# Seven block products in place of eight in the up projections of a streaming encoder

## What is computed

```
def conv_gated_mlp(xn, w_up, conv_w, conv_b, w_down):
    gate, val = jnp.split(xn @ w_up, 2, axis=-1)          # 1024 -> 2 x 2816
    return (jax.nn.silu(causal_dwconv(gate, conv_w, conv_b)) * val) @ w_down

h = h + conv_gated_mlp(rmsnorm(h, norm_ffn_g[layer]), ...)
```

## Time and profile before

| | |
|---|---|
| median of three runs | 1069.85 us |
| the profiled execution's own time | 1069.4 us |
| its span (first to last instruction) | 1067.6 us |
| TensorE (PE), busy share of the span | 99% |
| VectorE (DVE) | 59% |
| ScalarE (ACT) | 44% |
| GpSimd (POOL) | 17% |
| TensorE's granted clock | 0.999 of full speed |

### The profile page before, as it was taken

One profiled execution on the slowest core, in us unless ns is written; L12 is line 12 of the kernel. 1 busy time (PEld: TensorE's weight loads), 2 busy tenths in 40 slices (PEclk: granted clock), 3 DMA queues, 4 the chain that ended last, 5 costly groups with the idle time before them and its releaser, 6 DMA issues.

```text
span 1067.6 us, 15530 instructions
## 1 busy us (share of the span) xinstructions
PE 1057.9 (99%) x5552; PEld 866.9 (81%) x5552; DVE 631.7 (59%) x876; ACT 464.9 (44%) x733; POOL 184.8 (17%) x245
## 2 busy tenths in 40 slices
PE   9999999999999999999999999999999999999997
PEld 8887778888888888888888777888888888888886
DVE  6798755666666666633335774756666666643332
ACT  6456664544344444422323665554443444422221
POOL 8998911300000000000000221310000000000000
PEclk9999999999999999999999999999999999999999
DMA  6551025133222222223233111322222222222322
GB/s 231 168 128 41 14 91 197 61 130 106 98 97 85 97 94 98 99 99 118 98 111 135 61 60 41 118 99 98 87 97 93 96 98 98 98 99 99 119 80 79
DMA packets 36460, 107.27 MB, mean 100 GB/s; under 512 B 7809, under 2 KB 10113, under 8 KB 36161
## 3 DMA queue, kind: packets, MB, share of 16 engines
q1 hardware_dynamic: 36416, 106.69, 29.4%
HBM read 102.09 MB, written 3.15 MB: 99 GB/s over the span
## 4 chain that ended last, share of the span: by engine, by line
PE 95%; DVE 2%; ACT 1%; SPq 1%; DMA 1%; issue 1%; POOL 0%; DVEq 0%; ACTq 0%
PE bank L1596 30%; PE bank L1597 29%; PE bank L1598 29%; PE bank L1620 2%; PE bank L1986 1%; PE bank L1963 1%; DMA raw<-wstream 1%; PE bank L1743 1%; PE bank L1808 1%; DVE ssum L1090 0%; SPq L360 0%; PE bank L1707 0%; PE bank L1687 0%; DVE wlo L1057 0%; PE bank L1771 0%
## 5 line engine op out<-in xcount | busy, mean ns | idle before, releaser
L1596 PE MATMUL bank<-xhi,whi 128*128 128x512 f32 x960 | 376.1, 392 | 0.2 <-DVE wlo L1057 0.2
L1597 PE MATMUL bank<-xlo,whi 128*128 128x512 f32 x960 | 373.7, 389 | 0.0
L1598 PE MATMUL bank<-xhi,wlo 128*128 128x512 f32 x960 | 373.6, 389 | 0.0
L1057 DVE TENSOR_TENSOR wlo<-raw,whi 128x1024 fp32r<-128x1024 f32 x177 | 224.7, 1271 | 206.6 <-ACT whi L702 206.2
L702 ACT ACTIVATE whi<-raw 128x1024 fp32r<-128x1024 f32 x177 | 187.2, 1058 | 324.0 <-PE bank L1598 300.4
L1596 PEld LDWEIGHTS bank<-xhi,whi 128*128 128x128 f32 x960 | 180.2, 188 | 39.6 <-issue 0.8
L1598 PEld LDWEIGHTS bank<-xhi,wlo 128*128 128x128 f32 x960 | 180.2, 188 | 37.8
L1597 PEld LDWEIGHTS bank<-xlo,whi 128*128 128x128 f32 x960 | 180.3, 188 | 36.9 <-issue 0.2
L1596 PE MATMUL bank<-ahi,whi 128*128 128x512 f32 (+1 forms) x374 | 141.0, 377 | 0.0
L1598 PE MATMUL bank<-ahi,wlo 128*128 128x512 f32 (+1 forms) x374 | 140.8, 377 | 0.0
L1597 PE MATMUL bank<-alo,whi 128*128 128x512 f32 (+1 forms) x374 | 140.8, 377 | 0.0
(11 more groups left out here) (264 smaller groups left out, 1051.5 us busy)
## 6 DMA issues: line engine op xcount, KB each, us to landing
raw<-wstream SPq DMA_DIRECT2D x177, 512.0 KB, 3.2
xin<-xT SPq DMA_DIRECT2D x8, 256.0 KB, 5.7
raw<-wstream SPq DMA_DIRECT2D x8, 256.0 KB, 5.2
h<-xT SPq DMA_DIRECT2D x1, 2048.0 KB, 8.3
u_scratch<-uperm SPq DMA_DIRECT2D x1, 1024.0 KB, 5.6
uc<-u_scratch SPq DMA_DIRECT2D x8, 128.0 KB, 4.4
bandsb<-band SPq DMA_DIRECT2D x1, 1024.0 KB, 4.7
outT<-outb SPq DMA_DIRECT2D x2, 512.0 KB, 2.8
```

The costliest lines, as they stand in the source:

```text
L1057: V.tensor_tensor(wlo[:, t % RING, :], raw[:, t % RAWS, :], whi[:, t % RING, :].bitcast(f32), ALU.subtract).then_inc(lo_done, 1)
L1596: MM(dst, wh, rhi, start=start, stop=False)
L1597: MM(dst, wh, rlo, start=False, stop=False)
L1598: return MM(dst, wl, rhi, start=False, stop=stop)
```

## The change

Two of the 22 pairs stay as they were. The other twenty of each layer are formed with Strassen's scheme in Winograd's form. The product of a pair is seen as two by two blocks: the gate and value tiles, each cut into an upper and a lower half of the input columns (four blocks of 128 each), times the normed activations `xn`, cut by input half and by token half. Seven products ("quarters") of four blocks by 256 tokens take the place of eight.

- The sums of weights, `fold[0]` to `fold[3]`, and three kinds of residual are made on GpSimd: in each pair four sums of 128 by 512 (`pair_folds`, `pair_fold4`) and two residuals of 128 by 512 (`pair_fold4_lo`, `pair_keep_lo`).
- ScalarE makes the high parts (128 by 1024, 512, 1536 and 512 in each pair), takes the first product out of PSUM (`pair_p1`), and applies the first tap of the convolution (`pair_tap`), which was VectorE's.
- VectorE makes two residuals (128 by 1024 and 128 by 1536), adds the seven products up to the four parts of gate and value (`pair_u2`, `pair_u4`, `pair_row`), does the two other taps, and gates.
- The activations must be normed before the first quarter product, since their sums are formed ahead: `xn` on VectorE, four sums of them (128 by 1024, `turned_x`) on GpSimd, high parts of seven operands on ScalarE, residuals of six on VectorE and of one on GpSimd. All of this is placed beside the four plain products at the start of each up projection.
- The high part and residual of the gated result are no longer made pair by pair: they are made in groups of one to four blocks at the end (`a_high`, `a_low`), since the space is taken until then.
- The weights of a pair come in one load of 1 MB, with the value tile's halves swapped.

Core of the diff (the names of the waits tell who waits for whom):

```
# TensorE
+        def quarter(dst, slot, name):
+            hi, lo = XQ[name]
+            for b in range(4):
+                wh, wl = shi[:, slot, b * P:(b + 1) * P], slo[:, slot, b * P:(b + 1) * P]
+                MM(dst, wh, hi[:, b, :], start=b == 0, stop=False)
+                MM(dst, wh, lo[:, b, :], start=False, stop=False)
+                ins = MM(dst, wl, hi[:, b, :], start=False, stop=b == 3)
+            return ins
+        def period(p):
...
+            pe.wait_ge(cut_lo, p.one(1))
+            quarter(bank_p1, p.slot(0), "b11").then_inc(front_ready, 1)
+            quarter(p2_p6[:, 0, :], p.slot(1), "b21").then_inc(front_ready, 1)
+            pe.wait_ge(fold_lo, p.one(1))
+            quarter(p2_p6[:, 1, :], p.slot(2), "t2").then_inc(p6_ready, 1)
+            quarter(p5_p7[:, 0, :], p.slot(3), "t1")
+            quarter(p5_p7[:, 1, :], p.slot(4), "t3").then_inc(p7_ready, 1)
+            pe.wait_ge(fold4_lo, p.one(1))
+            quarter(p3_p4[:, 0, :], p.slot(5), "b22")
+            pe.wait_ge(keep_lo, p.one(1))
+            quarter(p3_p4[:, 1, :], p.slot(6), "t4").then_inc(p4_ready, 1)
...
# GpSimd
+        def pair_folds(p):
...
+            pool.wait_ge(pair_in[p.par], p.loaded())
+            if p.i is not None or p.c:
+                pool.wait_ge(fold_lo, p.one(0))
+            G.tensor_tensor(fold[:, 1, :], a21, a22, ALU.add).then_inc(fold_made, 1)
+            G.tensor_tensor(fold[:, 2, :], a11, a21, ALU.subtract)
+            pool.wait_ge(fold_made, p.three(0, 1))
+            G.tensor_tensor(fold[:, 0, :], fold[:, 1, :], a11, ALU.subtract).then_inc(fold_made, 1)
...
+                for c in (-1, 0):
+                    p = Pair(l, c, i)
+                    pair_folds(p.next())
+                    pair_fold4_lo(p)
+                    pair_fold4(p.next())
+                    pair_keep_lo(p.next())
+            pair_fold4_lo(Pair(l, NPAIR - 1))
+            for j0, j1, group in A_POOL:
+                a_low(l, j0, j1, group)
...
# ScalarE
+        def period(p):
+            pair_tap(p.prev())
+            pair_p1(p)
+            pair_fold4_hi(p)
+            pair_silu(p.prev())
+            pair_gate_hi(p.next())
+            pair_keep_hi(p.next())
+            pair_fold_hi(p.next())
...
# VectorE
+        def period(p):
+            pair_row(p.prev())
+            pair_conv(p.prev())
+            pair_gated(p.prev())
+            pair_u2(p)
+            pair_gate_lo(p.next())
+            pair_u4(p)
+            pair_fold_lo(p.next())
...
+            pair_u2(last)
+            split_lo(d0)
+            a_low(l, 0)
+            pair_u4(last)
+            a_low(l, 1)
+            split_lo(d0 + 1)
+            pair_row(last)
+            a_low(l, 2)
+            pair_conv(last)
+            a_low(l, 3)
+            pair_gated(last)
+            a_low(l, 4)
+            split_lo(d0 + 2)
+            a_low(l, 5)
+            split_lo(d0 + 3)
```

More of the change, by code:

```diff
@@ L47 @@
 T_OUT = 23
[L48 to L49 removed]
+T_UP = [27, 73]
+T_DN = [T_UP[0] + 4, T_UP[1] + 4]
 T_QKV = T_DN[0] + 3 * KB
@@ L102, in used_count, with __init__, count, one @@
     return t + 1 if t < T_QK else t if t < T_GLU else t - 2
+class Pair:
+    def __init__(self, l, c, i=None):
+        self.l, self.c, self.i, self.par = l, c, i, c % 2
+    def count(self, d, each, k):
+        c = SEEN + each * (NPAIR * self.l + self.c + d) + k
+        return c if self.i is None else self.i * (2 * each) + c
+    def one(self, d):
+        return self.count(d, 1, 0)
+    def two(self, d, k):
+        return self.count(d, 2, k)
+    def three(self, d, k):
+        return self.count(d, 3, k)
+    def done(self, d, each=1, k=0):
+        c = each * (FJ * self.l + PLAIN + self.c + d) + k
+        return c if self.i is None else self.i * (2 * each) + c
+    def loaded(self):
+        c = 16 * (NPAIR // 2 * self.l + self.c // 2 + 1)
+        return c if self.i is None else self.i * 16 + c
+    def prev(self):
+        return Pair(self.l, self.c - 1, self.i)
+    def next(self):
+        return Pair(self.l, self.c + 1, self.i)
+    def block(self):
+        return PLAIN + self.c if self.i is None else self.i * 2 + (PLAIN + self.c)
+    def slot(self, k):
+        if k == 6:
+            k += self.par
+        return (2 * (T_UP[self.l] % RING) + k) % (2 * RING)
 class Steps:
@@ new lines, in pair_fold4, with pair_fold4_lo @@
+        def pair_fold4(p):
+            pool.wait_ge(fold_made, p.three(0, 2))
+            if p.i is not None or p.c:
+                pool.wait_ge(fold4_lo, p.one(0))
+            G.tensor_tensor(fold[:, 3, :], raws[p.par][:, 0, 4 * P:], fold[:, 0, :], ALU.subtract).then_inc(fold_made, 1)
+        def pair_fold4_lo(p):
+            pool.wait_ge(fold_hi, p.two(0, 2))
+            G.tensor_tensor(slo[:, p.slot(5), :], fold[:, 3, :], shi[:, p.slot(5), :].bitcast(f32),
+                            ALU.subtract).then_inc(fold4_lo, 1)
@@ L1395, in attended_residual @@
             row_sum_lo(n)
-            dve.wait_ge(rstd_done, n + 1)
[L1398 to L1431, removed]
-                    V.tensor_tensor(alo[:, i * 2 + jj, :], abuf[:, :], ahi[:, i * 2 + jj, :].bitcast(f32),
-                                    ALU.subtract).then_inc(alo_done, 1)
-            steps.leave(FJ // 2)
@@ L2079, in mlp @@
         out = []
-        for j in range(FJ):
+        for j in range(PLAIN):
             out += [up[j], up[FJ + j]]
@@ L2097 @@
     wstream = np.ascontiguousarray(np.stack(stream))
+    spairs = []
+    for l in range(2):
+        up = _tiles(a["ffn_w_up"][l])
+        for j in range(PLAIN, FJ):
+            value = up[FJ + j]
+            spairs.append(np.stack([up[j], np.concatenate([value[:, 4 * P:], value[:, :4 * P]], axis=1)], axis=1))
+    spairs = np.ascontiguousarray(np.stack(spairs))
     def pairs(v):
```

372 lines of the change are left out of this document (347 added, 25 removed).

## The result

The changed kernel takes 1156.74 us (median of four runs, 1155.25 to 1158.28) against 1069.67 for the kernel before: a ratio of 1.0813, 95% interval 1.0799 to 1.0826. It is slower by 87 us; 1162 was forecast. The profiled execution has a span of 1154.1 (before 1067.6).

What follows compares the result with a forecast made beforehand. TensorE bounded the kernel; after the change, GpSimd and VectorE operations excluding each other would. Each layer 23.7 + 29.2 + 9.6 - 16.0 = +46.5, so 1069.4 + 93 = 1162.4, said as 1162 us; own range 1130 to 1190.

Steps and rivals of the forecast that it cites:

- 1052: Rival for the whole kernel: exclusion decides nothing, the loop runs at 10.08 and the saving comes through, 1052 us; chance 0.09.
- Exclusion with 0.14 given back: GpSimd and VectorE operations, the latter with both operands in SBUF, exclude each other; each change of hands returns some 0.14 us.
- nothing given back: Rival in the up projections: the lock holds for whole instructions, period 12.93, time 1201 us; chance 0.08.
- The loop: Pair loop: eleven GpSimd and VectorE operations stand in line, period 11.8 us against TensorE's 10.08; 17 periods cost +29.2 a layer.
- The walk: Step through one loop period, operation by operation from a fold residual's end: 12.93 less eight changes of hands, 11.8 us.
- The floor: Lower bound of the loop's period, with ten changes of hands: 11.5 us.
- TensorE's quarter: Seven products of 256 columns take 10.08 us a pair instead of 10.88, saving 16.0 us a layer; a quarter is 1.44.
- The head: Start of each up projection: both engines' work in line delays the first pair's P3 to 255.4 us; +23.7 a layer.
- The tail: End of each up projection: VectorE's late tile 2 residual, at 27.0, holds up seven down blocks; +9.6 a layer.
- a fall of the clock: Under the rival with period 12.93: TensorE's clock could fall in the head's waits of up to 9 us, costing some us.
- The sum: Each layer 23.7 + 29.2 + 9.6 - 16.0 = +46.5 us, with layer 1 taken to be like layer 0.
- only the loop is bound: Rival: head and tail cost only 7.4 together, the loop 29.2, a layer; 1111 us in all; chance 0.15.

Runs made afterwards that it cites:

- write_only: Changed kernel with GpSimd's operations in the up projections replaced by fills of about the same length, all waits kept: 1035.82 us, ratio 0.9683.
- before_tt: Kernel before, plus six unused GpSimd additions of 128 by 512 on two SBUF operands beside each pair: 1133.64 us, ratio 1.0597.
- before_ms: Kernel before, plus six unused GpSimd fills of 128 by 1536 beside each pair: 1069.68 us, ratio 0.9999.
- psum_conv: Changed kernel with the convolution's sum and silu's result of the Strassen pairs in two PSUM banks: 1109.82 us, ratio 1.0376.
- head_order: Changed kernel with the norm's factor also in PSUM and the start of each up projection reordered, first pair's P3 weights earlier: 1147.32 us, ratio 1.0722.
- all_psum: Changed kernel with start and end reordered, and convolution's sum, silu's result and a second copy of the gate tile's high part in PSUM: 1071.8 us.
- sums_dve: halves with the activation sums t1 and t3 made on VectorE instead of GpSimd: 1069.94 us, ratio 1.0007.
- halves: all_psum with GpSimd's 128 by 1024 operations at start and end of each up projection cut into two of 128 by 512: 1071.17 us.

## Why the prediction was right, point by point

- **Time, sign and place.** 1156.7 against 1162, inside the own range of 1130 to 1190. The main forecast holds; each of the rivals is off by 44 or more (1052, 1111, 1201).
- **Exclusion with 0.14 given back.** Shown by the two timelines above and by write_only, before_tt, before_ms and psum_conv. With nothing given back the loop would run at 12.93.
- **The loop: 11.8 forecast, 11.56 measured.** The walk's order is that of the trace. Mis-sized is what the changes of hands give back: the walk has eight at 0.14 and one at 0.08, 1.2 together; the trace has nine at 0.13 to 0.21, 1.4 together. 16 x 0.24 = 3.8 a layer too much. The floor stated was 11.5.
- **TensorE's quarter: 10.08 a pair forecast, 9.89 and 9.52 measured** in an unbroken loop (write_only). The sign is right, the saving is 19.8 and 27.2 a layer and not 16.0. In the kernel after it bought nothing, since TensorE waits in every pair.
- **The head: +23.7 forecast.** P1 near 232: 232.98. P3 near 255.4: 255.26. P6 of the third pair at 275.0: its weights were ready at 271.93, but it started at 278.4, because P3 and P4 of the second pair began at 270.36 and ran at half clock (5.3 for 2.8). What counts is the line of the two engines. The third fold residual ended 3.1 before the forecast's 275.0 because it went ahead of two of GpSimd's operations (they end at 273.06 and 274.29), and these stood in line behind it: the fourth ended at 286.53, where the forecast has 275.0 + 11.8 = 286.8. An agreement of 0.3 is closer than the walk's rounded terms ("say 5" for the load, "some 28 changes of hands") can promise, so some of it is luck.
- **The tail: +9.6 forecast, +10.4 measured** (32.6 from the last fold residual's end, 471.53, to the end mark, for 22.2). Tile 2's residual came at 26.2, forecast 27.0; the wait is 5.23 for "about 5". The seven blocks behind it took 6.3 for 4.8, with a granted clock of 0.63 between 497.8 and 502. The prediction named a fall of the clock under a rival and for the head only; it belonged into the tail's sum. So the tail's 0.8 off is two errors that partly cancel, -0.8 and +1.5.
- **The sum.** Layer 0: +46.5 forecast, -0.3 in the head, -3.8 in the loop, +0.8 in the tail give +43.2; measured +43.5. Layer 1 was taken to be like it, and in sum it is, +43.05, but in other parts: counted from where TensorE enters the up projection, its norms and its fourth fold residual are 2.1 earlier than in layer 0, and its tail is 34.3 and not 32.6 long, since tile 2's residual comes 1.0 later and the blocks behind it run longer at half clock. No term of the forecast has either. The marker of the earlier trace rows would have hidden this, with 45.0 and 42.5.
- **The range.** Its lower end adds up to 17 + 24.1 + 6 - 16 = +31 a layer, not +32; the measured +43 lies well inside either way.
- **Rival "only the loop is bound".** Wrong: head and tail cost what the line of both engines says, and in head_order a large gap ahead of P3 was removed and only half of it reached the loop.
- **What would make it wrong:** no wait of TensorE for loads appears, and the period isn't 10.1.

The Trainium skill (SBUF — State Buffer, Who interferes with whom) says of a VectorE instruction with two SBUF inputs that it contends with a GpSimd instruction that reads SBUF, "not with one that only writes it". before_tt and before_ms agree, 1509 ns against 752. It calls the shared ports an exclusive lock and says, of VectorE's modes with two ports, that the loser "fully blocks"; the trace of the two-operand forms agrees in kind, with 0.13 to 0.21 us given back at each change. It says too that an instruction with at most one SBUF input, outside those modes, doesn't contend: psum_conv and all_psum agree for the taps (755 ns) and the residual of the gate tile. And it names `tensor_scalar` among the operations that can take the shared pair of ports by themselves; before_ms agrees, see the last section.

## What to carry to other kernels

Work moved to an idle GpSimd isn't beside VectorE's work but in line with it, wherever GpSimd reads SBUF and VectorE's operation has two SBUF operands: add up both engines' such operations before believing either's busy share. If that sum exceeds the bound, move one operand of each of VectorE's operations to PSUM: with two reorderings (worth 7 and 9 alone) this gave back 85 of 87 us, and no work was taken away. It did not make the new scheme faster than the old one. And where a pipeline starts and ends, removing a wait shows only where the next one is: what counts there is the work in line, and here head and tail took back all that the loop saved.

## What the runs showed of the hardware that was not expected

- 256-column matmuls stand 0.1178 apart in layer 0 and 0.1133 in layer 1 of write_only, at the same granted clock, with the same program of TensorE and much the same load on the others; the earlier trace rows have 0.120 in a short stretch. 7.4 us in twenty pairs hang on it, nearly as much as lies between that kernel's two runs (1031.57 and 1040.08; the profiled one took 1040.08). It doesn't belong to a layer: in layer 0 of the kernel after the matmuls from 296.06 to 302.29 stand 0.1133 apart, and the first after the wait at 304.17 0.118 and more. What sets it is open.
- In the kernel after, TensorE came back at half its clock, the 1.2 of 1.2 and 2.4 GHz, from every wait of 2.6 to 7.7 us. With waits of 1.3 to 1.6 in nearly every period of the loop the granted clock stayed 1.00. The wait's length alone doesn't decide: after 3.41 us the clock fell in layer 0 of sums_dve (236.49) and stayed 1.00 in its layer 1 (727.42). Two windows of the kernel after, columns as in the earlier trace rows:

```profile
232.00:236.00 4.00, 2.90 (x12) 2.63 (x12) 4.00 (x2) 0.00 (x0) 3.06 (x1) 0.50 0.00 0
...
252.00:256.00 4.00, 0.74 (x3) 0.74 (x4) 2.35 (x2) 3.12 (x4) 3.86 (x4) 0.50 0.00 2
```

In the head of the kernel after it cost next to nothing, as other work was waited for (the forecast without it is 0.3 off); in its tail 1.6 and 2.2 us in the two layers, and in halves 2.6 at one place.
- A fill on GpSimd, which reads nothing, doubles VectorE's `TENSOR_SCALAR` (547 to 1166 ns) and leaves its taps with two SBUF operands at 752; adds on GpSimd, which double those, bring `TENSOR_SCALAR` only to 654.
